# Mixture-of-experts trunk: expert gate and up weights loaded two chunks wide, down weights two rows per partition

## The reference

```
def moe_ffn(h, w_router, wg, wu, wd):
    ...
    for e in range(N_EXPERTS):
        out = out + gate[:, e:e + 1].astype(hf.dtype) * swiglu(hf, wg[e], wu[e], wd[e])

def swiglu(h, wg, wu, wd):
    return (jax.nn.silu(h @ wg) * (h @ wu)) @ wd
```

## Time and profile before

| | |
|---|---|
| median of 3 runs | 1737.0 us (1736.01 to 1737.09) |
| span of the profiled execution (no other time of it is given) | 1734.0 us |
| TensorE matmul busy | 1709.9 us, 99% |
| TensorE weight loads | 1499.3 us, 86% |
| VectorE | 1277.4 us, 74% |
| ScalarE | 1058.2 us, 61% |
| GpSimd | 23.7 us, 1% |
| moved by DMA | 477.54 MB, mean 275 GB/s |
| packets | 213,216; 13,732 of them under 2 KB |
| mean granted TensorE clock | 0.993 |

### The profile page before, as it was taken

How to read it: one execution, slowest core, us unless ns; L and a number is a source line. 1 busy time by engine, 2 the same in 40 slices (tenths; PEclk the granted TensorE clock), 3 DMA queues, 4 the chain that set the end, 5 groups by cost and what they waited for, 6 DMA issues and landing times. The chain is left out here.

```text
span 1734.0 us, 24266 instructions
## 1 busy us (share of the span) xinstructions
PE 1709.9 (99%) x9681; PEld 1499.3 (86%) x9681; DVE 1277.4 (74%) x935; ACT 1058.2 (61%) x852; POOL 23.7 (1%) x56
## 2 busy tenths in 40 slices
PE   8999999999999999899999999999999999999997
PEld 7999889989899989788888888888888888888886
DVE  5555655454565564698898898888888898988986
ACT  5443555343454454477777777777777777777774
POOL 1000000000000010100000000000000000000000
PEclk9999999999999999999999999999999999999998
DMA  9555634465665553899999999999999999999970
GB/s 325 191 173 170 223 124 159 152 219 165 207 194 177 183 187 122 291 336 368 340 369 363 336 365 362 340 365 367 338 370 367 332 358 370 338 370 343 359 274 24
DMA packets 213216, 477.54 MB, mean 275 GB/s; under 512 B 8516, under 2 KB 13732, under 8 KB 213156
## 3 DMA queue, kind: packets, MB, share of 16 engines
q1 hardware_dynamic: 213156, 476.69, 77.4%
HBM read 475.61 MB, written 1.05 MB: 275 GB/s over the span
## 5 line engine op out<-in xcount | busy, mean ns | idle before, releaser
L454 ACT ACTIVATE whi<-raw 128x2048 fp32r<-128x2048 f32 (+1 forms) x260 | 492.5, 1897 | 252.2 <-PE ps L1175 107.4
L1440 PE MATMUL ps<-whi,a_hi 128*128 128x512 f32 x1792 | 557.3, 392 | 0.0
L774 DVE TENSOR_TENSOR wlo<-raw_more,whi 128x2048 fp32r<-128x2048 f32 x192 | 436.9, 2289 | 52.9 <-ACT whi L454 52.9
L454 ACT ACTIVATE whi<-raw_more 128x2048 fp32r<-128x2048 f32 x192 | 368.8, 1921 | 124.8 <-PE ps L1440 70.9
L769 DVE TENSOR_TENSOR wlo<-raw,whi 128x2048 fp32r<-128x2048 f32 (+1 forms) x116 | 259.0, 2236 | 210.2 <-ACT whi L454 210.1
L1440 PEld LDWEIGHTS ps<-whi,a_hi 128*128 128x128 f32 x1792 | 332.8, 188 | 67.3
L774 DVE TENSOR_TENSOR wlo<-raw,whi 128x2048 fp32r<-128x2048 f32 x144 | 327.7, 2290 | 69.7 <-ACT whi L454 69.7
L1440 PE MATMUL ps<-wlo,a_hi 128*128 128x512 f32 x896 | 349.6, 390 | 0.0
L1175 PE MATMUL ps<-a_hi,whi 128*128 128x256 f32 x992 | 281.4, 284 | 0.0
L1175 PE MATMUL ps<-a_hi,wlo 128*128 128x256 f32 x992 | 280.7, 283 | 0.0
L1175 PE MATMUL ps<-a_lo,whi 128*128 128x256 f32 x992 | 280.7, 283 | 0.0
(11 more groups left out here) (208 smaller groups left out, 1681.5 us busy)
## 6 DMA issues: line engine op xcount, KB each, us to landing
raw_more<-in_w_e_down SPq DMA_DIRECT2D x80, 1024.0 KB, 6.2
raw<-in_w_e_gate SPq DMA_DIRECT2D x64, 1024.0 KB, 5.7
raw_more<-in_w_e_up SPq DMA_DIRECT2D x64, 1024.0 KB, 7.0
raw<-in_w_e_up SPq DMA_DIRECT2D x48, 1024.0 KB, 6.0
raw_more<-in_w_e_gate SPq DMA_DIRECT2D x48, 1024.0 KB, 6.5
raw<-in_w_in SPq DMA_DIRECT2D x32, 1024.0 KB, 5.2
raw<-in_w_e_down SPq DMA_DIRECT2D x32, 1024.0 KB, 6.5
raw<-in_w_xk SPq DMA_DIRECT2D x8, 1024.0 KB, 5.2
```

The costliest lines, as they stand in the source:

```text
L454: return act.activation(dst, src, ACT.Copy, scale=scale)
L774: return dve.tensor_tensor(dst, src, hi.bitcast(F32), ALU.subtract)
L1440: ins = pe.matmul(o, (heh, hel)[xi][:, 4 * part + k, :], w[wi][:, k, :], start=part == 0 and k == 0 and n == 0, stop=part == 1 and k == 3 ...
```

## The change

```
-        def expert_unit(i):
...
+        GROUPS = [(j, min(2, NJ - j)) for j in range(0, NJ, 2)]
...
+        for g in range(len(GROUPS)):
+            add_group("gate", g, GATE)
+            add_group("up", g, UP)
+            if g:
+                add_group("down", g - 1, DOWN)
+        add_group("down", len(GROUPS) - 1, DOWN)
...
+        for g, (j, n) in enumerate(GROUPS):
+            for c in range(n):
+                T_AFTER[j + c] = GATE[g + 1] + 2 * c if g + 1 < len(GROUPS) else DOWN[g] - 1
+        SCATTER_AFTER = (GATE[0] + 3, GATE[0] + 3, UP[0] + 3, GATE[1] + 3)
+        ST_AFTER = UP[1] + 3
...
                     if w == "down":
-                        src = a["w_e_down"][0][bass.ds(e, 1), (j * 4 + part * 2) * P:(j * 4 + part * 2 + 2) * P, :]
+                        k, kk = 4 * j + 2 * part, 2
+                        src = a["w_e_down"][0][bass.ds(e, 1), k * P:(k + kk) * P, :]
                     else:
-                        src = a["w_e_" + w][0][bass.ds(e, 1), part * C:(part + 1) * C, j * C:(j + 1) * C]
+                        kk = 4 // n
+                        k = kk * part
+                        src = a["w_e_" + w][0][bass.ds(e, 1), k * P:(k + kk) * P, j * C:(j + n) * C]
+                    rows_of = "e (p k) n -> p (e k) n" if w == "down" else "e (k p) n -> p (e k) n"
...
+                def slot_wait(i, v):
+                    if i != DOWN[0]:
+                        n = i + 1 if i == DOWN[0] - 1 else i
+                        sp.wait_ge(s["lo_ready"], v * BODY + (U0 + n - MR + 1))
...
+                def silu(j, v):
+                    if j >= 2:
+                        act.wait_ge(s["act_ready"], v * NJ + (j - 1))
+                    act.activation(silu_t[j % 2][:], bank(j % 2), ACT.Silu).then_inc(s["silu_ready"], 1)
...
+                        for g, (j, n) in enumerate(GROUPS):
+                            if i == UP[g] + 1:
+                                act.wait_ge(s["unit_used"], v * BODY + (U0 + UP[g]))
+                                for c in range(n):
+                                    silu(j + c, v)
+                        for j in range(NJ - 1):
+                            if i == T_AFTER[j] + 2:
+                                act_hi(j, v)
...
+                            end = UP[g] + 2 * n
+                            if i == end + 1:
+                                dve.wait_ge(s["unit_used"], v * BODY + (U0 + end))
+                                for c in range(n):
+                                    dve.wait_ge(s["silu_ready"], v * NJ + (j + c + 1))
+                                    if j:
+                                        dve.wait_ge(s["t_done"], v * NJ + (j + c - 1))
+                                    dve.tensor_tensor(act_t[c][:], silu_t[c][:], bank(2 + c), ALU.mult
+                                                      ).then_inc(s["act_ready"], 1)
...
+                        if i == ST_AFTER + 2:
...
+                    if part == 0 and w_name == "gate" and g:
+                        pe.wait_ge(s["silu_ready"], v * NJ + GROUPS[g][0])
...
+                        for c in range(n_c):
                             for n, (wi, xi) in enumerate(PASSES):
-                                ins = pe.matmul(o, (heh, hel)[xi][:, 4 * part + k, :], w[wi][:, k, :],
+                                ins = pe.matmul(bank(b0 + c), (heh, hel)[xi][:, kt, :], w[wi][:, k, c * C:(c + 1) * C],
...
+                    rows_of = act_t[j % 2][:].rearrange("s (b p k) -> s b k p", b=2, k=2)
                     for f in range(4):
-                        ins = pe.transpose(bank(6)[:, f * P:(f + 1) * P], act_t[:, f * P:(f + 1) * P], ident[:])
+                        ins = pe.transpose(bank(6)[:, f * P:(f + 1) * P], rows_of[:, f // 2, f % 2, :], ident[:])
```

More of the change, by code:

```diff
@@ L150, in trunk @@
     rs = place("rsum_s", [P, DEPTH, NH, NT], F32)
+    act1 = place("act_tok1", [P, C], F32)
     assert at["top"] <= nc.sbuf_usable_end, (at["top"], nc.sbuf_usable_end)
@@ L193, in trunk @@
     ones = moe("ones", [P, P], F32)
-    silu_t = moe("silu_tmp", [P, C], F32)
-    act_t = moe("act_tok", [P, C], F32)
+    silu_t = [moe("silu_tmp", [P, C], F32), place("silu_tmp1", [P, C], F32, place_of["w_group"])]
+    act_t = [moe("act_tok", [P, C], F32), act1]
     rev = moe("rev_index", [P, NT, NE], F32)
@@ L263, in cols, with add_group @@
             return ap[:, :, c * C:(c + 1) * C]
-        def expert_unit(i):
[L267 to L279, removed]
+        GROUPS = [(j, min(2, NJ - j)) for j in range(0, NJ, 2)]
+        GATE, UP, DOWN, order = [0] * len(GROUPS), [0] * len(GROUPS), [0] * len(GROUPS), []
+        def add_group(w, g, first):
+            first[g] = len(order)
+            for part in range(2 * GROUPS[g][1]):
+                order.append((w, g, part))
+        for g in range(len(GROUPS)):
[4 more added lines that the diff above has]
+        add_group("down", len(GROUPS) - 1, DOWN)
+        assert len(order) == BODY
+        T_AFTER = {}
+        for g, (j, n) in enumerate(GROUPS):
[3 more added lines that the diff above has]
+        ST_AFTER = UP[1] + 3
         def u_free(c):
@@ L348, in load_first @@
                     for i in range(MR):
[L350 removed]
+                        slot_wait(i, v)
                         load_expert_unit(i, e)
@@ L1453, in act_t_, with down @@
                     ins.then_inc(s["t_done"], 1)
-                def down(j, i0, v):
+                def down(i, v):
+                    _, g, part = order[i]
+                    j = GROUPS[g][0] + part // 2
                     pe.wait_ge(s["actT_ready"], v * NJ + (j + 1))
[L1458 to L1470, removed]
+                    u = U0 + i
+                    pe.wait_ge(s["lo_ready"], v * BODY + (u + 1))
+                    w = [t[u % SPL][:, :].rearrange("p (k n) -> p k n", k=2) for t in (whi, wlo)]
+                    for k in range(2):
+                        f = 2 * (part % 2) + k
+                        for c in range(2):
+                            for n, (wi, xi) in enumerate(PASSES):
+                                ins = pe.matmul(bank(4 + c), (aTh, aTl)[xi][j % 2][:, f, :],
+                                                w[wi][:, k, c * C:(c + 1) * C],
+                                                start=j == 0 and f == 0 and n == 0,
+                                                stop=j == NJ - 1 and f == 3 and n == 2)
+                    ins.then_inc(s["unit_used"], 1)
@@ L1486, in _ @@
                 with pe.Fori(0, visits) as v:
[L1487 to L1500, removed]
+                    for i in range(BODY):
+                        if order[i][0] == "down":
+                            down(i, v)
+                        else:
+                            gate_up(i, v)
+                        for n in range(4):
+                            if i == SCATTER_AFTER[n]:
+                                if n == 0:
+                                    pe.wait_ge(s["y_ready"], v + 1)
+                                if n >= 2:
+                                    pe.wait_ge(s["xadd_done"], v * 4 + n)
+                                scatter(n, v)
+                        if i == ST_AFTER:
                             pe.wait_ge(s["xadd_done"], v * 4 + 4)
@@ L1509, in _ @@
                             ins.then_inc(s["ts_done"], 1)
[L1510 to L1514, removed]
+                        for j in range(NJ):
+                            if i == T_AFTER[j]:
+                                act_t_(j, v)
+                        if i == DOWN[-1] - 1:
+                            gather(v + 2)
         PIECES = [(c, t) for t in range(NT) for c in range(2)]
```

74 lines of the change are left out of this document (30 added, 44 removed).

## The result

The change takes 1739.13 us (median of 20 runs, 1738.13 to 1740.23) against 1736.24 (20 runs, 1735.56 to 1737.35): a ratio of 1.0016, 95% interval 1.001 to 1.0022. The forecast was 1739.1, from a base of 1737.0; the 20 new runs put the base 0.8 lower, so the change cost 2.9 us where 2.1 were forecast. It is slower by less than the 0.2% that the prediction called telling. The size came out well, but about a third of it for a reason that the prediction had set to nothing.

The account below looks back on a forecast made before the run. The prediction took TensorE to bound the expert stage. Two stalls of 0.17 to 0.36 us a visit, times 8, middle 2.1 us, on a base of 1737.0 gave 1739.1 us, range 1736.5 to 1746.5.

Parts of the forecast that it names:

- TensorE bounds the stage, the loads don't: Expert stage: TensorE's matmuls fill each 123.8 us visit; loads are 30 us ahead, so changing them costs 0.
- The rival that rested on the DMA share: Expert stage bound by loads after all: longer transfers save 43 us, giving 1694; chance 0.06.
- The strided transposes cost nothing: TensorE's transposes of act_tok, now reading every second element: taken as 0 out of 0 to 20 us.
- the prediction's own signs: For slow transposes: act_tok's weight load above 139 ns or its group of transposes longer than 0.35 us.
- The rival's 20 us: Strided transposes at half speed: 0.35 us more per group, 20 us in all, 1759 with the stalls; chance 0.13.
- Place one: Before unit 26 (third pair's up units): VectorE's wlo 0.05 us late plus restart, stall 0.17 to 0.28 us a visit.
- The hole of "0.3 to 0.6 us" among its signs: Sign of being right: a TensorE hole of 0.3 to 0.6 us once per visit before unit 26.
- Place two: Unit 18 (down, after the gate transposes): VectorE's second product delays wlo, stall 0 to 0.08 us a visit.
- The sum: Both stalls together, 0.17 to 0.36 us a visit, times 8: 1.4 to 2.9 us, middle 2.1.
- Further stalls: Rival: units 15, 18, 26, 30 and 38 late, 6 to 10 us, about 1745; chance 0.12.
- no cost: Rival: hand-overs faster than taken cover both late places, units 26 and 18, giving 1737.0; chance 0.14.

Follow-up runs that it names:

- run 6: The change with only half of each unit loaded in the expert stage, but for the first fourteen, against the old kernel: 1739.47 us, ratio 1.0017.
- run 3: The change with gate transposes behind unit 23 and the old down-row layout, against the old kernel: 1736.82 us, ratio 1.0004; second time 1736.40 us, 1.0001.
- run 4: The old kernel with only the down rows paired (8192-byte runs, stride-two transposes), against the old kernel: 1737.68 us, ratio 1.0007.
- run 2: The change with the old layout of the down rows, so transposes read neighbouring columns, against the old kernel: 1738.17 us, ratio 1.0013.
- run 1: The change with gate transposes and next selection behind unit 23 instead of unit 15, against the old kernel: 1737.61 us, ratio 1.0009.
- run 7: The change with one more silu on ScalarE ahead of the third pair's two, against the old kernel: 1744.70 us, ratio 1.0048.
- run 8: The old kernel with the last chunk's transposes moved between the two gate units, against the old kernel: 1743.73 us, ratio 1.0042.
- run 5: The change with four neighbouring down rows per partition, so transposes read every fourth column, against the old kernel: 1738.99 us, ratio 1.0015.
- run 9: The old kernel with the gate transposes moved right ahead of chunk 3's transposes: 1735.79 us against 1736.40, ratio 0.9996.

## Why the prediction was right, and where not

- *TensorE bounds the stage, the loads don't.* Right. Half the bytes change nothing (run 6), and pairs with 4096-byte runs give 1.0001 (run 3, second time). The rival that rested on the DMA share had 0.06.
- *The strided transposes cost nothing.* Wrong: this is the step that failed. It inferred from TensorE's steady pace that reading had room, and took 0 of a range of 0 to 20 us. By the prediction's own signs the transposes did get slower: 204 ns a load, a group longer than 0.35 us. The load takes 65 ns more, nearly half its time, but most of that passes beside other work: the group grew by 0.03 us, by some 0.02 with the matmuls behind it, and the visit by 0.14 (run 4) or, taken out of the change, by 0.10 (run 2). Eight visits: 0.8 to 1.1 us, at the low end of the range, and not the end itself. The rival's 20 us had the opposite fault, for it let the whole group double with its loads. The trace had the hint: four loads of 139 ns are 0.56 us and the group took 0.35, so part of each load was hidden.
- *Place one, 0.17 to 0.28 us a visit.* Right in place and cause (runs 1, 7, 8), and with 0.17 at the lower end of the range, but its terms were off to both sides. It took the low part to end 0.05 us after TensorE wants it; it ended 0.03 before (806.15 against a steady start at 806.18). It took the start to cost 0.08 in the matmul behind it; 0.11 stand there and 0.03 more in the rest of the unit. The hole of "0.3 to 0.6 us" among its signs is found only as the two gaps of 0.26 and 0.34 taken together. ScalarE began its silu 0.20 us after TensorE went on (800.74 to 800.94), where the old order had 0.27 (1047.14 in the earlier trace rows to 1047.41 in the earlier trace rows). The old order had two semaphore values to work out ahead of its silu and the new one has one, which may be why. Run 8, with the old order on ScalarE, has 0.28 again (801.18 to 801.46) and a unit late by 0.11 and not 0.03, which fits; no run tested it by itself. And VectorE's hand-over took 0.06 us, near the lower end of the 0.04 to 0.15.
- *Place two, 0 to 0.08.* Nothing was lost, the lower end.
- *The sum, 1.4 to 2.9.* Measured on the visits: 8 x 0.30 = 2.4 us. The medians differ by 2.9, with an interval of 1.7 to 3.8 us. In the two profiled executions another 0.6 lies ahead of the first visit, where the first gather starts at 726.72 and 727.29 (its row in the old kernel's timeline, in the change's, and in those of runs 1, 5 and 9):

```profile
726.72 3.74 PE L1425 MATMUL ps<-sel_tok,h_tok 128*128 128x128 f32 x32
727.29 3.74 PE L1447 MATMUL ps<-sel_tok,h_tok 128*128 128x128 f32 x32
728.05 3.74 PE L1447 MATMUL ps<-sel_tok,h_tok 128*128 128x128 f32 x32
726.81 3.74 PE L1451 MATMUL ps<-sel_tok,h_tok 128*128 128x128 f32 x32
727.77 3.74 PE L1425 MATMUL ps<-sel_tok,h_tok 128*128 128x128 f32 x32
```

  Up to there runs 1 and 5 have the change's code and lie on both sides of it, and run 9 has the old kernel's and is 1.05 later than it. So this part is put down to the execution and not to the change.
- *Further stalls, no cost.* Neither: one hole a visit, no second.

That the visits' 2.4 us are so near the 2.1 is in part luck: holes taken 0.10 us a visit too large (0.27 in the middle for both places, 0.17 measured) stood against a stride taken 0.10 too small. The last 0.03 of a visit's 0.30 is what run 3 has over the old kernel with neither; its cause is open.

## What to carry to other kernels

Where an engine is fed by a chain with fixed slots, write down for each boundary how much of its own other work lies between two units: work that looks like overhead (here four transposes) can be the very time that lets the chain keep up, and moving it costs even if its amount stays. A DMA share near 1 says how full the engines look, not that anybody waits: ask who waits for a load, or halve the loads. And an operand's stride is to be priced as a number of its own, even if its time is hidden.

## What was not expected of the hardware

A TensorE weight load of 128 x 128 float32 values for a transpose takes 139 ns from neighbouring columns and 204 ns from every second or every fourth one (203): a step, not a slope. In a row of four transposes the 65 ns cost only 0.03 us in all. And a start after a wait has a price of its own: whether TensorE was held up for 0.03 us (the change), 0.11 (run 8) or 0.66 (run 7), the unit behind took 0.13 to 0.17 us more than a steady one, 0.11 of it in the gap behind the late matmul. So a wait of 0.03 us cost 0.17.
